# Decay sums formed once and split, and spread per head by a short-format product: a two-block model on one Trainium2 core

## What is computed

```python
dt = softplus(dt + dt_bias)                      # [token, head]
a  = -exp(a_log)                                 # [head]
a_cum = cumsum(dt * a, axis=token)               # in each chunk of 128
seg   = a_cum[i] - a_cum[j]                      # for each head
decay = exp(where(j <= i, seg, -inf))
cb    = einsum('bcign,bcjgn->bcijg', cm, bm)
y_diag = einsum('bcijg,bcijgr,bcjgrp->bcigrp', cb, decay, xdt)
...                                              # carried state, skip, gate, group norm, out product
```

## Time and profile before

| | us |
|---|---|
| runs | 1051.25, 1050.33, 1058.77 |
| median | 1051.25 |
| profiled execution, whole | 1057.03 |
| its span, first to last instruction | 1055.2 |

### The profile page before, as it was taken

One profiled execution on the slowest core, in us unless ns is written; L12 is line 12 of the kernel. 1 busy time (PEld: TensorE's weight loads), 2 busy tenths in 40 slices (PEclk: granted clock), 3 DMA queues, 4 the chain that ended last, 5 costly groups with the idle time before them and its releaser, 6 DMA issues.

```text
span 1055.2 us, 14425 instructions
## 1 busy us (share of the span) xinstructions
PE 963.6 (91%) x5761; PEld 838.2 (79%) x5761; DVE 692.3 (66%) x945; ACT 528.3 (50%) x785; POOL 62.3 (6%) x65
## 2 busy tenths in 40 slices
PE   4989999999989979999997998898897988789898
PEld 4887897888868769999886998777776867667676
DVE  4579636863887678888636867755554767765555
ACT  4654322232543456655435557647653565543453
POOL 6002312310000000000000000000000000000000
PEclk9899999999999989999998999999998999889899
DMA  9442222122544546555554454422223444420042
GB/s 297 125 143 93 81 76 85 41 81 82 168 149 160 164 138 198 187 175 197 191 173 157 122 163 153 144 103 80 81 89 120 149 141 165 155 79 1 1 160 80
DMA packets 80531, 135.78 MB, mean 129 GB/s; under 512 B 3893, under 2 KB 46225, under 8 KB 80336
## 3 DMA queue, kind: packets, MB, share of 16 engines
q1 hardware_dynamic: 78640, 131.37, 38.0%
q0 software_dynamic: 1824, 3.48, 1.1%
HBM read 133.79 MB, written 1.05 MB: 128 GB/s over the span
## 4 chain that ended last, share of the span: by engine, by line
PE 56%; ACT 9%; DVE 8%; issue 5%; DMA 1%; DVEq 0%; ACTq 0%
PE bank L421 15%; PE bank L423 15%; PE bank L422 15%; ACT upper L1142 3%; PE bank L409 3%; DVE lower L1603 2%; PE bank L1002 1%; PE bank L1017 1%; PE bank L994 1%; ACT arena L1204 1%; PE bank L835 1%; ACT arena L1446 1%; ACT L1446 1%; DVE arena L2077 1%; DMA loaded<-in_ffn_w_up 1%
## 5 line engine op out<-in xcount | busy, mean ns | idle before, releaser
L1603 DVE TENSOR_TENSOR lower<-loaded,upper 128x2048 fp32r<-128x2048 f32 (+1 forms) x123 | 279.1, 2276 | 161.9 <-ACT upper L1142 159.9
L1142 ACT ACTIVATE upper<-loaded 128x2048 fp32r<-128x2048 f32 (+1 forms) x123 | 233.0, 1899 | 144.8 <-PE bank L423 123.6
L421 PE MATMUL bank<-xT_upper,upper 128*128 128x256 f32 x656 | 188.8, 288 | 9.7 <-DVE xT_lower L1644 9.7
L422 PE MATMUL bank<-xT_lower,upper 128*128 128x256 f32 x656 | 187.0, 285 | 0.0
L423 PE MATMUL bank<-xT_upper,lower 128*128 128x256 f32 x656 | 186.8, 285 | 0.0
L421 PE MATMUL bank<-upper,xT_upper 128*128 128x512 f32 (+1 forms) x368 | 151.0, 410 | 9.2 <-DVE lower L1603 6.7
L423 PE MATMUL bank<-upper,xT_lower 128*128 128x512 f32 (+1 forms) x368 | 145.2, 395 | 0.0
L422 PE MATMUL bank<-lower,xT_upper 128*128 128x512 f32 (+1 forms) x368 | 144.2, 392 | 0.0
L421 PEld LDWEIGHTS bank<-xT_upper,upper 128*128 128x128 f32 x656 | 127.6, 195 | 11.5 <-issue 11.5
L1204 ACT ACTIVATE arena<-bank 128x512 f32<-128x512 f32 (+1 forms) x95 | 54.0, 587 | 160.4 <-PE bank L634 62.7
L421 PE MATMUL bank<-upper,split_arena 128*128 128x512 f32 x296 | 122.8, 415 | 11.0 <-DVE split_arena L1644 4.5
(11 more groups left out here) (306 smaller groups left out, 1258.8 us busy)
## 6 DMA issues: line engine op xcount, KB each, us to landing
loaded<-in_w_in SPq DMA_DIRECT2D x27, 1024.0 KB, 5.2
loaded<-in_ffn_w_up SPq DMA_DIRECT2D x22, 1024.0 KB, 5.2
loaded<-in_ssm_in_w SPq DMA_DIRECT2D x20, 1024.0 KB, 5.3
loaded<-in_ffn_w_down SPq DMA_DIRECT2D x11, 1024.0 KB, 5.0
loaded<-in_ssm_out_w SPq DMA_DIRECT2D x8, 1024.0 KB, 5.0
loaded<-in_ple_gate_w SPq DMA_DIRECT2D x8, 1024.0 KB, 5.1
loaded<-in_attn_in_w SPq DMA_DIRECT2D x8, 1024.0 KB, 5.2
loaded<-in_w_branch_ret SPq DMA_DIRECT2D x4, 1024.0 KB, 5.0
```

Of the source, the lines that this page charges most:

```text
L421: mm(out, a[0], b[0], start=start, stop=False)
L422: mm(out, a[0], b[1], start=False, stop=False)
L1142: A(part(upper, PARTS, n), part(loaded, LOADS, n), ACT.Copy).then_inc(uppers, 1)
L1603: TT(part(lower, LOADS, n), part(loaded, LOADS, n), part(upper, PARTS, n).bitcast(F32), sub) \
```

## The change

Before, each spread computes the running sums of its 4 heads anew from `adt`. Now they are formed once, transposed (head along the partitions, token along the columns), for all 32 heads and both chunks:

- VectorE writes `adt2`, which is `adt` twice side by side (64 columns), so that the transposed sums come out twice, in partitions 0 to 31 and 32 to 63.
- TensorE forms them with two more fp32 products in the ("ac",) group; that group's bank now carries 352 columns in use.
- VectorE copies them to `decays` in fp32r (rounded: the upper part), and then overwrites partitions 32 to 63 by the remainder (sum minus upper part). It also forms `pick`: 64 rows by 32 columns, with a one at row h and at row 32 + h of column h.
- In `spread`, the stationary operand is column hd of `pick`, broadcast to 128 columns, and the moving one is `decays`: 64 rows, fp32r. Its product adds upper part and remainder of head hd in every row.
- The bank of ("ac",) is emptied by the last of VectorE's new instructions, and TensorE waits for that once more before the first spread.

```diff
--- before.py
+++ after.py
@@ -180,6 +180,8 @@
         lora_at = (nc.sbuf_base + 31) // 32 * 32
         lora = sb("lora", [P, 2, 512])
         masks = nc.alloc_sbuf_tensor_at("masks", [P, 2, P], F32R, offset=lora_at)
+        decays = nc.alloc_sbuf_tensor_at("decays", [P, 2, P], F32R, offset=lora_at + 4 * 512)
+        pick = nc.alloc_sbuf_tensor_at("pick", [P, 32], F32R, offset=lora_at + 4 * 768)
         postw = sb("postw", [P, D])
         rowp = sb("rowp", [P, 64 + 64 + 16 + 32 * 3])
         h = sb("h", [P, 2, D])
@@ -291,6 +293,7 @@
         dtv, adt, acs = sm(200, 2, 32), sm(264, 2, 32), sm(328, 2, 32)
         tot, dte, eac = sm(392, 32), sm(424, 32), sm(456, 32)
         arow = sm(488, 32)
+        adt2 = sm(1160, 2, 64)
         nacs = sm(136, 2, 32)
         ang, cosd, sind = sm(520, 4, 32), sm(648, 4, 64), sm(904, 4, 64)
         angn = sm(1160, 4, 32)
@@ -803,7 +806,10 @@
                     ps = take(pe, ("ac",), 6)
                     for n in range(2):
                         mm(ps[:, 32 * n:32 * n + 32], const("incl"), adt[:, n, :], start=True, stop=True)
-                    fill(mm(ps[:, 64:96], const("ones"), adt[:, 0, :], start=True, stop=True), ("ac",))
+                    mm(ps[:, 64:96], const("ones"), adt[:, 0, :], start=True, stop=True)
+                    for n in range(2):
+                        last = mm(ps[0:64, P + P * n:2 * P + P * n], adt2[:, n, :], const("incl"), start=True, stop=True)
+                    fill(last, ("ac",))
 
             z_keys = lambda j: [("z", j, i) for i in range(2)]
             z_banks = {}
@@ -832,7 +838,7 @@
                    masks[:, 1, :].unsqueeze(1).broadcast_to([P, 4, P]), start=True, stop=False)
                 for e in range(4):
                     hd = 8 * g + 4 * hf + e
-                    last = mm(ps[:, P * e:P * e + P], adt[:, n, hd:hd + 1].to_broadcast([P, P]), const("incl"),
+                    last = mm(ps[:, P * e:P * e + P], pick[0:64, hd:hd + 1].to_broadcast([64, P]), decays[0:64, n, :],
                               start=False, stop=(e == 3))
                 fill(last, ("bc", z))
 
@@ -899,6 +905,7 @@
             states(3)
             z_piece(1, 1, 1)
             pe.wait_ge(sem("masks_ready"), 1)
+            emptied(pe, ("ac",))
             spread(0)
             spread(1)
             pe.wait_ge(sem("xd_ready"), 3)
@@ -2056,6 +2063,8 @@
                 ve.wait_ge(sem("dt_log"), 1)
                 link(TT(dtv[:, :, :], dtv[:, :, :], adt[:, :, :], add))
                 link(TS(arow, arow, -1.0, None, mul))
+                for c in range(2):
+                    link(TT(adt2[:, :, 32 * c:32 * c + 32], dtv[:, :, :], bc(arow.unsqueeze(1), P, 2, 32), mul))
                 TT(adt[:, :, :], dtv[:, :, :], bc(arow.unsqueeze(1), P, 2, 32), mul).then_inc(sem("adt_ready"), 1)
 
             def step_sums():
@@ -2063,7 +2072,11 @@
                 v = ps[:, 0:64].rearrange("p (a b) -> p a b", a=2)
                 link(ve.tensor_copy(acs[:, :, :], v))
                 link(TS(nacs[:, :, :], v, -1.0, None, mul))
-                empty(TT(tot, ps[:, 64:96], acs[:, 0, :], sub), ("ac",))
+                link(TT(tot, ps[:, 64:96], acs[:, 0, :], sub))
+                w = ps[0:64, P:3 * P].rearrange("p (a b) -> p a b", a=2)
+                link(ve.tensor_copy(decays[0:64, :, :], w))
+                link(TT(pick[0:64, :], ident[0:64, 0:32], ident[0:64, 32:64], add))
+                empty(TT(decays[32:64, :, :], w[32:64], decays[32:64, :, :].bitcast(F32), sub), ("ac",))
                 emptied(ve, ("ac",))
                 ve.nop().then_inc(sem("dte_in"), 1)
```

## The result

| | before | after |
|---|---|---|
| median, us | 1052.79 (20 runs, 1044.39 to 1062.29) | 1056.94 (20 runs, 1055.46 to 1065.39) |
| profiled execution, us (span) | 1057.03 (1055.2) | 1056.3 (1054.5) |
| granted clock over the profiled span | 0.956 | 0.952 |

The account below looks back on a forecast made before the run. The prediction took the chain through VectorE's step_sums in the convolution, and through TensorE, ScalarE and VectorE in the scan, as the bound. +1.1 - 0.6 = +0.5 us on a median of 1051.25 gave 1051.8 us, range 1048.0 to 1056.5.

Parts of the forecast that it names:

- Step (a): Convolution, step_sums: three new VectorE instructions ahead of the release of bank 6 lengthen the chain, +1.1 us.
- (b): step_logs: two more VectorE products ahead of the one TensorE awaits cost nothing; 0.5 us without cover.
- (c): TensorE at ("ac",): two more fp32 products, about 0.45 and at most 0.9 us, cost nothing, covered by a wait.
- (e): Before the first spread: TensorE's new wait for bank 6 is met 40 us earlier, so no cost.
- Step (d): Scan's 16 spreads, 8 on the chain: each falls only from 1.13 to 1.06 us because of borders, -0.6 us.
- Rival 1: Scan's spreads: the borders of the 64-row products cost nothing, so -2.5 us in all, 1048.8 us; chance 0.10.
- rival 3: Scan's spreads: the short format at 128 columns is no faster than fp32, so +3.7 us, 1055.0 us; chance 0.06.
- The sum: Convolution's +1.1 us and the scan spreads' -0.6 us give +0.5 us, 1051.8 us; chance 0.52.
- How the numbers follow: The prediction's passage giving the chances of the sum and of its rivals, the forecast 1051.8 us and the range.
- rival 2: Scan's spreads: one or two more falls of the clock add 1.6 to 3.2 us, 1053.4 to 1055.0 us; chance 0.22.

Follow-up runs that it names:

- rows128: The changed kernel with the spreads' products on 128 rows, rows 64 to 127 of decays and pick being zeros: 1055.99 us, 1.0028 of the kernel before.
- after_again: The changed kernel measured once more, unaltered: 1057.01 us, 1.0028 of the kernel before.
- scan_fill2: The changed kernel with 2 dense products, results overwritten, in TensorE's wait at the scan's start: 1057.29 us, 1.0056 of the kernel before.
- before_gap: The kernel before with two of the four products left out in each of spreads 0 and 1: 1056.93 us, 1.0040 of the kernel before.
- the filled version: The changed kernel with transposed sums formed late off the chain, 128-row spreads, and dense products in both waits: 1048.42 us, and 1046.54 us when repeated.
- conv_only: The changed kernel with the old fp32 spreads from adt; the new sums are formed but unread: 1053.75 us, 1.0004 of the kernel before.

## Why the prediction was wrong

**Step (a)** held: 1.12 us on the chain for 1.1, 0.43 + 0.20 + 0.43 where it had 0.44 + 0.22 + 0.44. The transposes run behind them as it said.

It also said that the wait of 3.4 us grows by all of it; the wait grew by 0.2 us, since its start moved too, and the cost on the chain is the full 1.12 us all the same.

**Steps (b), (c) and (e)** held as far as the profile shows: TensorE waits 3.6 us for bank 6, and for nothing of these steps. (c) measures 0.70 us, inside its 0.45 to 0.9. They were not tried by themselves.

**Step (d)** held in its mechanism. A spread takes 1.03 us for the 1.06 foreseen, with both borders there, and without them (rows128) 0.68. 8 x -0.10 = -0.8 for -0.6. The Trainium skill's rule from page TensorEngine Tiling, section Key Properties, that a switch of the tiling mode drains TensorE, agrees with the trace: 0.35 us for the two borders of a spread. Rival 1 fell by the first timeline, and rival 3 with it (four records in 0.39 to 0.59 us).

**The sum** of +0.5, with the measured (d) +0.3, is borne out as far as the fitted rate can be trusted: with the clock taken out, the two sets of the changed kernel give -0.2 and 0.0, standard errors 0.6 and 0.8.

**What failed is that the sum put the clock at nothing.** How the numbers follow took rival 2, one or two more falls, at 0.22, beside a sum at 0.52 that left the clock as it was. The runs show 10 us more half clock than in the kernel before (99.3 to 89.3), which at 0.32 are 3.2 us, and one stretch of the scan longer by 1.5 us (after_again) or 3.0 us (the changed kernel's first trace). So rival 2's mechanism was right, and its 1.6 to 3.2 us were about right as well. Its chance was wrong, and so was its place. I looked for the fall inside the spreads and in the grown wait of step (a). It came, in every trace with shorter spreads and an unfilled wait, behind a wait on ScalarE at the scan's start. That wait grew from 1.0 to 1.4 us because spreads 0 and 1, which are not on the chain, take 0.42 us less together (691.71 to 694.13 before, 690.92 to 692.92 now). The argument against it ("between them the stream is dense") does not hold at the scan's start. Whatever TensorE saves ahead of that wait becomes idle time, and the clock of what follows is lower. Not all of the 10 us lie there: the falls behind this wait are 3.4 to 6.7 us long, and where the rest comes from is open.

**A smaller part** is the base: I put the sum on the median of three runs, 1051.25. Twenty gave 1052.79, 1.5 us more. That alone brings the forecast to 1053.3 and leaves 3.6 us of miss. With it the top of the range would have been 1058.0, above the measured time; the time would still have stood 3.6 us above the sum, and 3.2 of them go with the clock.

What the lower clock costs was taken as 8 products x 0.2 us a fall, 1.6 us. Spread 2 to 3 bears that out: 1.6 us more in scan_fill2 and before_gap, whose falls have 3.4 us of half clock, and 3.1 in the changed kernel, whose fall has 6.7. The page TensorE: Matmul & The Clock Gate of the Trainium skill, section Terms, puts the penalty at the time at the lower level times one less the ratio of the clocks, here half. On this stretch, which is TensorE's alone, the traces are close to it (0.46 to 0.48). By that estimate the 10 us of the whole span would cost 5.0. The runs have 0.32 a us, less than that; the page of the profile gives TensorE 57% of the chain, which would explain it, but no run shows this. The measurement decides.

Open are four things: what about the new spreads makes a wait of 0.74 us enough, why rows128 stands 1.7 us above its steps, why the filled version gains 1 us more than its own, and what the other stretches at half clock (some 80 us in every kernel) hang on. One profile for each kernel can't say how often each of these comes.

## What to carry to other kernels

Work that TensorE saves just ahead of a wait on another engine gained nothing here (3.4 us from spread 0 to 2 whatever stood between), and cost time through the clock of the stretch behind that wait. Before pricing a TensorE edit, list the waits that it lengthens, the short ones too, and see whether dense work can be moved (or useless dense products put) into them. Where runs of one kernel differ by 10 us, take the time at the lower clock out of each run first, with a rate fitted over all runs, and look for a stretch of the trace that the edit must shorten; an edit of 1 or 2 us can show then, where it is lost in the medians. A product on part of the rows between full ones cost its two borders (0.35 us), so a row count that matches its neighbours can be worth more than the rows saved.

## What the runs showed that I had not expected

- Leaving four products out of the kernel before made it slower: 1056.93 against 1051.54 us (before_gap).
- A wait of 0.74 us, with 64-row spreads and two dense products ahead of it and such a spread behind it, had the lower clock behind it (0.86 over 690 to 702, scan_fill2), where waits of 0.98 us behind 128-row fp32 products had not (1.00 in before, conv_only).
- Executions of one kernel on one chip ranged from 1042.26 to 1064.36 us (the kernel before, 35 runs). Within a kernel the span goes with the half clock, with a correlation of 0.8 in the kernel before.
- A split of 64x256 out of a bank takes 0.43 us on VectorE, and so does the difference of 32x256: as long as 128x256.
